# Mixed attention's differential units: the relative bias is added by VectorE within its row maxima, instead of by TensorE with identity products

## The chip, the cores and the metric

The kernel runs on one core of a Trainium2 chip. The metric is the device time of one execution in microseconds (us): the median of several. A core has four engines that compute: TensorE (PE: matrix products into the PSUM memory, with a separate part that loads weights, PEld), VectorE (DVE), ScalarE (ACT) and GpSimd (POOL); SyncE (SP) issues DMA transfers. Each engine works through its own list of instructions in order, and waits for others through semaphores.

## What is computed

Two model blocks follow each other on 256 tokens of width 1024. The first has four layers (dilated attention twice, a short convolution, a conformer convolution, each with a gated feed-forward part). The second adds 16 meta tokens (272 keys) and has a feed-forward part, a mixed attention and another feed-forward part. The change lies in the mixed attention, in its differential half:

```python
bias = bias_a[rel_bucket(q_pos[:, None], k_pos[None, :])].transpose(2, 0, 1)
s = jnp.einsum('bqhmd,bkhmd->bhmqk', q[:, start:stop], k[:, :stop]).astype(jnp.float32)
s = s * A_SCALE + bias[None, :, None].astype(jnp.float32)
s = jnp.where(k_pos[None, :] <= q_pos[:, None], s, -jnp.inf)
p = jax.nn.softmax(s, axis=-1)
a = p[:, :, 0] - lam * p[:, :, 1]
outs.append(jnp.einsum('bhqk,bkhd->bqhd', a.astype(v.dtype), v[:, :stop]))
```

Each of 4 heads has two maps of scores (m = 0, 1) that share one bias; both get a softmax, and their difference weighs the values. The other half of the mixed attention (4 latent heads) works on keys picked by an index and has one map a head.

## The kernel before

Almost all time is matrix products of activations with weights. The weights are streamed from HBM in slabs, and each slab is split by ScalarE (L1260) and VectorE (L1689) into a high and a low part, so that three fast products (L2304 to L2306) give fp32 accuracy. The phases stand in one list (`phases`), and every engine's program runs over it; the order within a phase is written out by hand, the same on each engine's side.

The mixed attention is the phase `mix2`. It has 16 units: n = 0 to 7 are differential, n = 8 to 15 latent. `unit(n)` gives the query block q (units 0 to 3 and 8 to 11 are q = 0 with w = 144 keys, the others q = 1 with w = 272) and the head. Three buffers of scores in PSUM (`SCORE_BANK`, two banks for a differential unit, one a map) and three buffers of weights in SBUF (`expd`) are used in turn. For a differential unit n:

- `mix_scores` (TensorE): for each map a product of the identity with the bias table `rel2` (fp32, in SBUF; it holds bias and causal mask), L901, and on top of it the product of queries and keys, L905. A product of fp32 operands shows as two passes in the profile, so a unit has four rows of either line.
- `mix_max` (VectorE): one reduction over both maps gives the negative row maxima, L921.
- `mix_exps` (ScalarE): the exponential of each map, from PSUM into `expd`, with the row sums, L941.
- `weigh` (VectorE): reciprocals (L1002), times lambda (L1003, L1004), and the difference of the maps (L1005).
- `turn` (TensorE): two or three transposes with the identity, L1078; `turned_copy` (ScalarE): their copy to SBUF, L954.
- `values` (TensorE): the product with the values, L1095; `clamp` (VectorE): its bounded copy, L1013.

In the loop over n, VectorE does the maxima of unit n + 1, the weights of unit n, for n below 5 two steps of the index selection of the latent half (`select`, L819 to L823), then the clamp of unit n - 1. At n = 5 a reciprocal (L1044) stands ahead of the clamp. TensorE does the scores of unit n + 2, the values of unit n - 1 and the transposes of unit n. ScalarE does the exponentials of unit n + 1 and the copy of unit n's transposes. GpSimd makes eight sums of bias and selection for the latent units (L2271) as soon as the selection is there. Unit 0's scores, maxima and exponentials and unit 1's scores stand in the phase before, `heads`, between its last matrix products.

Latent units have their scores at L910, an add of the bias at L926, maxima at L929, and the values' product at L1097. The dilated attention of the first block has, at L559, a `tensor_tensor_reduce` that adds a mask to scores in PSUM, writes the negative sum to SBUF and takes the minimum of each row.

Of the kernel before, what the change touches and what calls it, by code (L numbers as in the profile page):

```python
# [23 lines left out]
ALU = mybir.AluOpType  # L24
ACT = mybir.ActivationFunctionType
AX = mybir.AxisListType.X
# [4 lines left out]
TW = SEQ + META  # L31
# [134 lines left out]
def build(nc, A, out):  # L166
# [81 lines left out]
    s = 0  # L248
# [59 lines left out]
    with ExitStack() as ctx:  # L308
        def sb(name, shape, dt=F32):
            return ctx.enter_context(nc.sbuf_tensor(name, shape, dt))  # L310

        def sem(name):
            return ctx.enter_context(nc.semaphore(name))
# [9 lines left out]
        rel2 = res[:].rearrange("p (h t) -> p h t", t=TW)  # L323
# [17 lines left out]
        def put(name, shape, offset, dt=F32):  # L341
            return nc.alloc_sbuf_tensor_at(name, shape, dt, offset=offset)
# [45 lines left out]
        z = put("z", [P, 20, TW], R_Q)  # L388
# [15 lines left out]
        ident = sb("ident", [P, P])  # L404
# [33 lines left out]
        ps = ctx.enter_context(nc.psum_tensor("ps", [P, 8, 512], F32))  # L438
# [16 lines left out]
        relw_ready, rel_done, skew_ready, skew_stored, bias_landed = (  # L455
            sem("relw_ready"), sem("rel_done"), sem("skew_ready"), [sem(f"skew_stored{j}") for j in range(2)],
            sem("bias_landed"))
# [42 lines left out]
        s2_done, s2_biased, s2_max, s2_exp, s2_prob = (  # L500
            sem("s2_done"), sem("s2_biased"), sem("s2_max"), sem("s2_exp"), sem("s2_prob"))
        t2_done, t2_copied, o2_done = sem("t2_done"), sem("t2_copied"), sem("o2_done")
# [122 lines left out]
        expd = [[tmp1[:, 2 * b + m, :] for m in range(2)] for b in range(3)]  # L625
# [14 lines left out]
        s2_negmax = [mstat[:, 40 + 2 * b:42 + 2 * b] for b in range(3)]  # L640
# [116 lines left out]
        def unit(n):  # L757

            return (n % 8) // 4, n % 4
# [131 lines left out]
        def mix_scores(pe, n):  # L891
            q, head = unit(n)
            w, bank = KEYS[q], SCORE_BANK[n % 3]
            if n == 0:
                pe.wait_ge(bias_landed, 32)
                pe.wait_ge(vl_copied, 3)
            if n >= 3:
                pe.wait_ge(s2_exp, n - 2)
            if n < 8:
                for m in range(2):  # L900
                    pe.matmul(ps[:, bank + m, 0:w], ident[:], rel2[:, head, TW - w:TW], start=True, stop=False,  # L901
                              skip_group_check=True)
                for m in range(2):
                    rows = slice(m * HD, (m + 1) * HD)
                    mm = pe.matmul(ps[:, bank + m, 0:w], z[rows, head, META + q * P:META + (q + 1) * P],  # L905
                                   z[rows, 4 + head, 0:w], start=False, stop=True, skip_group_check=True)
            else:
                pe.wait_ge(ckey_ready, 2)
                for k in range(2):
                    mm = pe.matmul(ps[:, bank, 0:w], qlat[:, 2 * head + k, q * P:(q + 1) * P], ckey[:, k, 0:w],  # L910
                                   start=(k == 0), stop=(k == 1))
            mm.then_inc(s2_done, 1)

        def mix_max(dve, n):
            q, head = unit(n)
            w, b, bank = KEYS[q], n % 3, SCORE_BANK[n % 3]
            dve.wait_ge(s2_done, n + 1)
            if n >= 3:
                dve.wait_ge(s2_exp, n - 2)
            if n < 8:  # L920
                dve.tensor_reduce(s2_negmax[b], ps[:, bank:bank + 2, 0:w], AX, ALU.max, negate=True).then_inc(s2_max, 1)  # L921
                return
            dve.wait_ge(bsel_ready, n - 7)
            dve.wait_ge(t2_done, n - 2)
            s = expd[b][0][:, 0:w]
            dve.scalar_tensor_tensor(out=s, in0=ps[:, bank, 0:w], scalar=rq[:, n - 8:n - 7], in1=bsel[:, n - 8, 0:w],  # L926
                                     op0=ALU.mult, op1=ALU.add).then_inc(s2_biased, 1)
            dve.wait_ge(s2_biased, n - 7)
            dve.tensor_reduce(s2_negmax[b][:, 0:1], s, AX, ALU.max, negate=True).then_inc(s2_max, 1)  # L929

        def mix_exps(act, n):
            q, _ = unit(n)
            w, b, bank = KEYS[q], n % 3, SCORE_BANK[n % 3]
            act.wait_ge(s2_max, n + 1)
            if n == 0:
                act.wait_ge(rq_sum, 1)
            if n >= 3:
                act.wait_ge(t2_done, n - 2)
            for m in range(2 if n < 8 else 1):
                src = ps[:, bank + m, 0:w] if n < 8 else expd[b][0][:, 0:w]  # L940
                e = act.activation(expd[b][m][:, 0:w], src, ACT.Exp, bias=s2_negmax[b][:, m:m + 1],  # L941
                                   accum_out=s2_sum[b][:, m:m + 1])
            e.then_inc(s2_exp, 1)

# [48 lines left out]
        def mix2_vector(dve, B, link):  # L993
# [39 lines left out]
            for n in range(16):  # L1033
                if n + 1 < 16:
                    mix_max(dve, n + 1)
                weigh(n)
                if n == TURN_BY_DVE:
                    turned_copy(dve, n).then_inc(t2_copied, 1)
                if n < 5:
                    for step in range(9 + 2 * n, min(11 + 2 * n, SEL_STEPS)):  # L1040
                        select(dve, step)
                if n == 5:
                    dve.wait_ge(rq_root, 1)
                    link(dve.reciprocal(rq, rq_std))  # L1044
                if 1 <= n <= 8:
                    clamp(n - 1)
                if n == 9:
                    dve.wait_ge(oa_sq, 8)
                    dve.tensor_scalar(oa_std, oa_sum, 1.0 / P, 1e-6 * OA_SCALE ** 2, ALU.mult, ALU.add).then_inc(oa_var, 1)
                if n == 10:  # L1050
                    dve.wait_ge(oa_root, 1)
                    link(dve.reciprocal(oa_rstd, oa_std))
                    link(dve.scalar_tensor_tensor(out=oa_rstd, in0=oa_std, scalar=OA_STD_MAX, in1=oa_rstd, op0=ALU.is_lt,
                                                  op1=ALU.mult))
                if n >= 13:
                    low_a(2 * (n - 13))
                    low_a(2 * (n - 13) + 1)
                if 10 <= n < 14:
                    scale_a(2 * (n - 10))
                    scale_a(2 * (n - 10) + 1)  # L1060
                if n >= 10:
                    low_b(n - 2)
# [5 lines left out]
        def mix2_tensor(pe, B):  # L1068
# [40 lines left out]
            for n in range(16):  # L1109
                if n + 2 < 16:  # L1110
                    mix_scores(pe, n + 2)
                if n == 0:
                    turn_values(pe, 2, B_heads)
                    turn_values(pe, 3, B_heads)
                if n:
                    values(n - 1)
                turn(n)
                if n >= 12:
                    turn_a(2 * (n - 12))
                    turn_a(2 * (n - 12) + 1)  # L1120
# [102 lines left out]
        def _(act):  # L1223
# [62 lines left out]
            for ph in phases:  # L1286
# [270 lines left out]
                elif ph.kind == "heads":  # L1557
                    for m in range(4 * ph.n):
# [29 lines left out]
                        if m == 15:  # L1588
                            latent_std(act)
                            load_table(act, ACT.Exp)  # L1590
                            mix_exps(act, 0)
# [10 lines left out]
        def _(dve):  # L1602
# [169 lines left out]
            for ph in phases:  # L1772
# [126 lines left out]
                elif ph.kind == "heads":  # L1899
# [7 lines left out]
                    for m in range(4 * ph.n):  # L1907
# [26 lines left out]
                        if m == 15:  # L1934
                            mix_max(dve, 0)
# [340 lines left out]
        def _(pe):  # L2276
# [80 lines left out]
            for ph in phases:  # L2357
# [263 lines left out]
                elif ph.kind == "heads":  # L2621
                    for m in range(4 * ph.n):
# [19 lines left out]
                        if m == 12:  # L2642
                            latent_query(pe, 6, B)
                            latent_query(pe, 7, B)
                            head_spreads(pe, 6)
                            head_spreads(pe, 7)
                        elif m == 13:
                            for k in range(3):
                                latent_values(pe, k)
                        elif m == 14:  # L2650
                            latent_sums(pe)
                            mix_scores(pe, 0)
                        elif m == 15:
                            turn_values(pe, 0, B)
                            turn_values(pe, 1, B)
                            pe.wait_ge(drained_a, B["da"] + 8)
                            mix_scores(pe, 1)
# [144 lines left out]
```

## Time and profile before

| | |
|---|---|
| median of 3 runs | 2153.34 us (2152.84 to 2155.52) |
| the profiled execution's own time | 2155.34 us |
| its span (first to last instruction) | 2153.5 us |
| mean granted clock of TensorE | 0.995 of full |
| TensorE busy | 2115.3 us (98%) |
| VectorE, ScalarE, GpSimd busy | 1477.2, 1018.1, 481.8 us |

The differential units lie between about 1885 and 1912 us from the start of the span, and the mixed attention ends at about 1932. Busy times are sums over the whole program; which engine sets the pace in a stage is read from its own stretch, and from the chain of waits, which is followed back from the last instruction: at each step to what released it, or to the instruction before it on its engine. A matrix product's bar overlaps that of the next one, and a VectorE bar overlaps the start of the next by some 0.08 us.

### The profile page before, as it was taken

How to read it: one execution, taken by the hardware profiler on the slowest of the kernel's cores; microseconds unless marked ns; L12 is line 12 of the kernel's file. 1: busy time of each engine (PE TensorE's matmuls, PEld its weight loads, DVE VectorE, ACT ScalarE, POOL GpSimd, SP SyncE). 2: the span in 40 equal slices, each digit the busy share in tenths (PEclk: the TensorE clock that was granted, in tenths of full speed). 3: DMA queues.
4: the chain of work that ended last, by engine and by line, in shares of the span. 5: the costliest groups of instructions: out<-in, count | busy, mean ns of one | idle time of the engine just before them, and what ended most of it. 6: DMA issues, size and time to landing. Idle time of an engine off the chain costs nothing.

```text
span 2153.5 us, 43259 instructions
## 1 busy us (share of the span) xinstructions
PE 2115.3 (98%) x16233; PEld 1935.1 (90%) x16240; DVE 1477.2 (69%) x2516; ACT 1018.1 (47%) x1376; POOL 481.8 (22%) x518
## 2 busy tenths in 40 slices
PE   8999999999999999999999999999999999999999
PEld 7997779989999888799889987799889998779998
DVE  7884778857688667688678847788565545586653
ACT  4335765544455443455543346655453334364342
POOL 3220005510135314044212200054113300201320
PEclk9999999999999999999999999999999999999999
DMA  5555235565645654245645563255655555305554
GB/s 184 192 177 185 89 124 175 190 202 174 211 138 192 202 161 148 69 158 193 208 154 190 180 190 104 97 181 181 200 163 171 172 172 178 98 21 176 181 182 144
DMA packets 300950, 350.37 MB, mean 163 GB/s; under 512 B 7604, under 2 KB 255990, under 8 KB 300854
## 3 DMA queue, kind: packets, MB, share of 16 engines
q1 hardware_dynamic: 295318, 344.45, 49.4%
q10 hardware_dynamic: 5152, 4.37, 0.7%
q8 instruction: 64, 1.05, 0.2%
q0 software_dynamic: 384, 0.24, 0.0%
q14 instruction: 32, 0.26, 0.0%
HBM read 346.35 MB, written 2.68 MB: 162 GB/s over the span
## 4 chain that ended last, share of the span: by engine, by line
PE 90%; DVE 4%; ACT 4%; issue 1%; DMA 0%; ACTq 0%; DVEq 0%
PE ps L2304 26%; PE ps L2306 26%; PE ps L2305 26%; PE ps L2731 2%; DVE w_lo L1689 2%; ACT w_hi L1260 1%; PE ps L2441 1%; PE ps L2436 1%; PE ps L2437 1%; ACT prob L566 1%; PE ps L2668 1%; PE ps L2373 1%; PE ps L2681 1%; PE ps L2316 1%; PE ps L2282 0%
## 5 line engine op out<-in xcount | busy, mean ns | idle before, releaser
L1689 DVE TENSOR_TENSOR w_lo<-raw,w_hi 128x2048 fp32r<-128x2048 f32 (+3 forms) x311 | 695.8, 2237 | 452.3 <-ACT w_hi L1260 452.2
L2304 PE MATMUL ps<-a_hi,w_hi 128*128 128x256 f32 (+1 forms) x3200 | 907.8, 284 | 6.3 <-DVE w_lo L1689 4.5
L2306 PE MATMUL ps<-a_hi,w_lo 128*128 128x256 f32 (+1 forms) x3200 | 904.4, 283 | 0.0
L2305 PE MATMUL ps<-a_lo,w_hi 128*128 128x256 f32 (+1 forms) x3200 | 904.2, 283 | 0.0
L1260 ACT CAST w_hi<-raw 128x2048 fp32r<-128x2048 f32 (+3 forms) x319 | 589.3, 1847 | 540.6 <-PE ps L2306 526.6
L2304 PEld LDWEIGHTS ps<-a_hi,w_hi 128*128 128x128 f32 x3200 | 605.8, 189 | 13.2 <-DVE w_lo L1689 6.4
L2306 PEld LDWEIGHTS ps<-a_hi,w_lo 128*128 128x128 f32 x3200 | 606.6, 190 | 0.0
L2305 PEld LDWEIGHTS ps<-a_lo,w_hi 128*128 128x128 f32 x3200 | 603.4, 189 | 0.4 <-issue 0.2
L2209 POOL TENSOR_TENSOR hs<-sg,cv 128x256 f32<-128x256 f32 x88 | 65.4, 743 | 644.4 <-DVE cv L2046 644.4
L2216 POOL CAST hid_hi<-hs 128x256 f32 (+3 forms) x132 | 137.9, 1045 | 297.0 <-DVE hs L2092 282.7
L2304 PE MATMUL ps<-w_hi,hid_hi 128*128 128x512 f32 x480 | 189.5, 395 | 2.3 <-DVE w_lo L1685 1.2
L2306 PE MATMUL ps<-w_hi,hid_lo 128*128 128x512 f32 x480 | 189.2, 394 | 0.0
L2305 PE MATMUL ps<-w_lo,hid_hi 128*128 128x512 f32 x480 | 188.4, 392 | 0.0
L1466 ACT ACTIVATE cv<-ps,par 128x256 f32<-128x256 f32 x176 | 82.1, 475 | 209.4 <-DVE ps L1735 205.1
L2046 DVE SCALAR_TENSOR_TENSOR cv<-ps,par,cv 128x255 f32<-128x255 f32 (+1 forms) x352 | 152.2, 477 | 27.1 <-ACT cv L1466 23.4
L2218 POOL TENSOR_TENSOR hid_lo<-hs,hid_hi 128x256 f32 (+3 forms) x132 | 138.1, 1046 | 20.9 <-POOL hid_hi L2216 19.9
L2248 POOL TENSOR_TENSOR qk<-rope_cos,rope_sin 128x256 f32 x96 | 79.0, 823 | 274.0 <-DVE rope_sin L1747 274.0
L1735 DVE TENSOR_TENSOR ps<-ps,rpre 128x256 f32<-128x256 f32 (+1 forms) x244 | 103.3, 429 | 36.4 <-PE ps L2306 30.2
L2304 PE MATMUL ps<-hid_hi,w_hi 128*128 128x256 f32 (+1 forms) x416 | 118.1, 284 | 0.3 <-DVE w_lo L1689 0.3
L2306 PE MATMUL ps<-hid_hi,w_lo 128*128 128x256 f32 (+1 forms) x416 | 117.9, 283 | 0.0
L2305 PE MATMUL ps<-hid_lo,w_hi 128*128 128x256 f32 (+1 forms) x416 | 117.6, 283 | 0.0
L2304 PEld LDWEIGHTS ps<-w_hi,hid_hi 128*128 128x128 f32 x480 | 90.2, 188 | 23.8 <-DVE w_lo L1685 2.0
(357 smaller groups left out, 2558.0 us busy)
## 6 DMA issues: line engine op xcount, KB each, us to landing
raw<-in_ffn_w_in_dram SPq DMA_DIRECT2D x88, 1024.0 KB, 5.1
raw<-in_attn_w_qkv_dram SPq DMA_DIRECT2D x71, 1024.0 KB, 5.1
raw<-in_ffn_w_out_dram SPq DMA_DIRECT2D x32, 1024.0 KB, 5.1
raw<-in_ffn_w_gate_dram SPq DMA_DIRECT2D x22, 1024.0 KB, 5.3
raw<-in_ffn_w_up_dram SPq DMA_DIRECT2D x22, 1024.0 KB, 5.3
raw<-in_ffn_w_down_dram SPq DMA_DIRECT2D x16, 896.0 KB, 4.9
raw<-in_sc_w_in_dram SPq DMA_DIRECT2D x12, 1024.0 KB, 5.2
raw<-in_ffn_w_out_dram SPq DMA_DIRECT2D x16, 768.0 KB, 4.5
```

Of the source, the lines that this page charges most:

```text
L1260: act.copy(o, src).then_inc(hi_ready, 1)
L1466: act.activation(cv[:, j, :], ps[:, j, 0:SEQ], ACT.Copy, scale=g).then_inc(tap_ready, 1)
L1689: dve.tensor_tensor(o, src, hi.bitcast(F32), ALU.subtract).then_inc(lo_ready, 1)
L1735: dve.tensor_tensor(tile, tile, rpre[:, 0:w], ALU.mult).then_inc(scaled, 1)
L2046: return dve.scalar_tensor_tensor(out=cv[:, j, back:SEQ], in0=ps[:, j, 0:SEQ - back], scalar=g, in1=cv[:, j, back:SEQ], op0=ALU.mult, op1= ...
L2209: pool.tensor_tensor(hs[:, j, 0:w], sg[:, j, 0:w], cv[:, 2 + j, :], ALU.mult).then_inc(hid_mul, 1)
L2216: pool.tensor_copy(hi, hs[:, j, 0:w]).then_inc(hid_hi_ready, 1)
L2218: pool.tensor_tensor(lo, hs[:, j, 0:w], hi.bitcast(F32), ALU.subtract).then_inc(hid_ready, 1)
L2248: pool.tensor_tensor(o, rope_cos[:, j, :], rope_sin[:, j, :], ALU.add).then_inc(rope_ready, 1)
L2304: pe.matmul(o, wh, xh, start=start, stop=False)
L2305: pe.matmul(o, wh, xl, start=False, stop=False)
L2306: return pe.matmul(o, wl, xh, start=False, stop=stop)
```

## The change

The identity products and TensorE's wait for the bias table are gone; queries times keys start the sum. VectorE runs, for each map, a `tensor_tensor_reduce` that reads the scores from PSUM and the bias from SBUF, writes -(scores + bias) into `expd` and the smallest value of each row into `s2_negmax`. It waits for the bias table at unit 0, and from unit 3 on for the transposes of unit n - 3, which read the same buffer. ScalarE's exponential reads `expd` in place with scale -1.

```diff
@@ mix_scores @@
             if n == 0:
-                pe.wait_ge(bias_landed, 32)
                 pe.wait_ge(vl_copied, 3)
             if n >= 3:
                 pe.wait_ge(s2_exp, n - 2)
             if n < 8:
                 for m in range(2):
-                    pe.matmul(ps[:, bank + m, 0:w], ident[:], rel2[:, head, TW - w:TW], start=True, stop=False,
-                              skip_group_check=True)
-                for m in range(2):
                     rows = slice(m * HD, (m + 1) * HD)
                     mm = pe.matmul(ps[:, bank + m, 0:w], z[rows, head, META + q * P:META + (q + 1) * P],
-                                   z[rows, 4 + head, 0:w], start=False, stop=True, skip_group_check=True)
+                                   z[rows, 4 + head, 0:w], start=True, stop=True, skip_group_check=True)
@@ mix_max @@
             if n < 8:
-                dve.tensor_reduce(s2_negmax[b], ps[:, bank:bank + 2, 0:w], AX, ALU.max, negate=True).then_inc(s2_max, 1)
+                if n == 0:
+                    dve.wait_ge(bias_landed, 32)
+                if n >= 3:
+                    dve.wait_ge(t2_done, n - 2)
+                for m in range(2):
+                    biased = dve.tensor_tensor_reduce(expd[b][m][:, 0:w], ps[:, bank + m, 0:w], rel2[:, head, TW - w:TW], -1.0,
+                                                      3.0e38, ALU.add, ALU.min, s2_negmax[b][:, m:m + 1])
+                biased.then_inc(s2_max, 1)
                 return
@@ mix_exps @@
             for m in range(2 if n < 8 else 1):
-                src = ps[:, bank + m, 0:w] if n < 8 else expd[b][0][:, 0:w]
-                e = act.activation(expd[b][m][:, 0:w], src, ACT.Exp, bias=s2_negmax[b][:, m:m + 1],
+                s = expd[b][m][:, 0:w]
+                e = act.activation(s, s, ACT.Exp, scale=-1.0 if n < 8 else 1.0, bias=s2_negmax[b][:, m:m + 1],
                                    accum_out=s2_sum[b][:, m:m + 1])
```

## Rows read from the trace of the kernel before

**Rows 1.** The page: the chain that ended last, share of the span by engine.

```profile
PE 90%; DVE 4%; ACT 4%; issue 1%; DMA 0%; ACTq 0%; DVEq 0%
```

**Rows 2.** Stretches: length, PE, PEld, DVE, ACT, POOL busy (count), PEclk, DMA share, GB/s.

```profile
1890.95:1904.50 13.55, 12.29 (x71) 7.95 (x71) 13.02 (x54) 8.12 (x32) 0.00 (x0) 1.00 0.00 1
1904.50:1910.50 6.00, 5.07 (x30) 3.60 (x30) 5.16 (x16) 3.47 (x14) 5.02 (x8) 1.00 0.00 0
```

**Rows 3.** The chain by line, from 1890.95 to 1910.50 and from 1910.50 to 1932.40.

```profile
by line: DVE mstat L921 16.2%; DVE tmp L1004 12.9%; DVE tmp L1005 12.8%; DVE chosen L823 12.3%; DVE top L821 11.3%; DVE mstat L1003 6.9%; issue 5.7%; PE ps L1095 5.5%; PE ps L901 4.7%; PE ps L905 3.4%; DVE tmp L1013 3.4%; DVE mstat L1002 2.
...
by line: PE ps L1097 31.9%; PE ps L1078 15.1%; PE ps L910 14.8%; ACT tmp L954 11.2%; PE ps L1095 10.3%; issue 4.1%; DVE mstat L929 2.0%; DVE tmp L954 1.9%; DVE tmp L926 1.9%; DVE tmp L1016 1.4%; DVE tmp L1009 1.4%; PE ps L1105 1.0%; DVE hid
```

**Rows 4.** The chain in order of time: start us, us, what.

```profile
1889.96 0.49 PE ps L901 x4
...
1904.49 0.49 PE ps L1078 x3
1904.99 0.92 PE ps L901 x4
...
1906.57 1.07 PE ps L1095 x6
...
1909.01 0.93 DVE tmp L1004
...
1911.05 0.49 ACT tmp L954
```

**Rows 5.** Waits of TensorE, whole program: us in total, times, longest.

```profile
PE ps L1078 <- DVE tmp L1005: 1.7, 3, 0.9
```

**Rows 6.** VectorE in order of time: start, us, line, operation, [idle before <- releaser].

```profile
1890.95 0.46 DVE L921 TENSOR_REDUCE mstat<-ps 128x2 f32<-128x288 f32 x1 [0.38 <-PE ps L905]
...
1893.62 0.45 DVE L921 TENSOR_REDUCE mstat<-ps 128x2 f32<-128x288 f32 x1
1893.99 0.15 DVE L1002 RECIPROCAL mstat<-mstat 128x2 f32<-128x2 f32 x1
...
1899.34 0.71 DVE L921 TENSOR_REDUCE mstat<-ps 128x2 f32<-128x544 f32 x1
1899.97 0.15 DVE L1002 RECIPROCAL mstat<-mstat 128x2 f32<-128x2 f32 x1
...
1906.91 0.19 DVE L1044 RECIPROCAL mstat<-mstat 128x8 f32<-128x8 f32 x1
1907.73 0.29 DVE L1013 TENSOR_SCALAR tmp<-ps 128x128 f32<-128x128 f32 x1 [0.63 <-PE ps L1095]
```

**Rows 7.** VectorE in the dilated attention, in order of time.

```profile
232.56 0.56 DVE L559 CUSTOM_DVE_ANT_0 prob<-ps,maskb 128x384 f32<-128x384 f32 x1 [0.58 <-PE ps L2324]
...
233.05 0.55 DVE L559 CUSTOM_DVE_ANT_0 prob<-ps,maskb 128x384 f32<-128x384 f32 x1
233.53 0.08 DVE L559 DVE_READ_ACCUMULATOR2_ANT cols<- 128x1 f32 x1
233.53 0.16 DVE L572 RECIPROCAL cols<-cols 128x1 f32<-128x1 f32 x1
```

**Rows 8.** Groups by line and shape, VectorE: count, busy us, mean ns, idle.

```profile
L1005 DVE SCALAR_TENSOR_TENSOR tmp<-tmp,mstat 128x272 f32<-128x272 f32 x4 | 2.1, 531 | 0.1
...
L926 DVE SCALAR_TENSOR_TENSOR tmp<-ps,mstat,bsel 128x272 f32<-128x272 f32 x4 | 2.0, 490 | 0.0
```

**Rows 9.** Line L941 on ScalarE: count, ns min/median/max, first and last start.

```profile
L941 ACT ACTIVATE tmp<-ps,mstat x16: 371/430/488, 1889.0 to 1909.2; 128x144 f32<-128x144 f32 x8, 128x272 f32<-128x272 f32 x8
...
L941 ACT ACTIVATE tmp<-tmp,mstat x8: 398/468/539, 1911.7 to 1927.4; 128x144 f32<-128x144 f32 x4, 128x272 f32<-128x272 f32 x4
```

**Rows 10.** VectorE's L1004 and GpSimd's last sum in order of time.

```profile
1903.54 0.36 DVE L1004 TENSOR_SCALAR tmp<-tmp,mstat 128x272 f32<-128x272 f32 x1
...
1909.01 0.76 POOL L2271 TENSOR_TENSOR bsel<-res,tmp 128x272 f32<-128x272 f32 x1
```

**Rows 11.** A stretch of the first block, columns as in rows 2.

```profile
302.50:305.00 2.50, 1.62 (x9) 1.23 (x9) 0.88 (x3) 1.79 (x5) 0.00 (x0) 0.77 0.29 110
```

## The prediction

> **What bounds the kernel now.** I read the page first. The chain that ended last is 90% TensorE [rows 1], so this is a TensorE-bound kernel with short stretches in which another engine sets the pace. The change touches one stage only, the 16 units of the mixed attention, so I asked next which engine paces that stage. The table of stretches shows VectorE busy for 13.02 of the 13.55 us from 1890.95 on, and for 5.16 of the next 6.00, while ScalarE has 8.12 and 3.47 [rows 2]. TensorE looks nearly as full there, 12.29 and 5.07, and a reader who stops at this table may think that work taken from it is worth its whole time. The chain of waits decides. By line it is almost all VectorE from 1890.95 to 1910.50: the row maxima (L921) alone are 16.2% of it, the identity products (L901) 4.7%; from 1910.50 to 1932.40 it is TensorE's, with the products of values (L1095, L1097), the transposes (L1078) and the scores of the latent units (L910), none of which the change touches [rows 3]. In order of time the identity products are on the chain in two places: just ahead of 1890.95, where unit 1's maxima wait for its scores, and at 1904.99, for unit 7 [rows 4]. Between them TensorE waits for VectorE instead: its transposes (L1078) stood idle until L1005 had written the weights, 3 times and 1.7 us in all [rows 5].
>
> **What it takes from TensorE.** Each differential unit loses two fp32 products with the identity, recorded as four passes: 0.49 us for 144 keys (units 0 to 3) and 0.92 us for 272 (units 4 to 7) [rows 4]. That is 4 x 0.49 + 4 x 0.92 = 5.6 us of TensorE in all. It is the most that the change can bring, and only if every pass were on the path.
>
> **What it adds to VectorE.** Before: one reduction over both maps. It keeps the engine 0.37 us at 144 keys (1893.62 until the reciprocal behind it starts, 1893.99) and 0.63 us at 272 (1899.34 to 1899.97) [rows 6]. After: two fused add-and-reduce instructions, one a map, each followed by a read of the accumulator. The trace has this pair, in the dilated attention at L559: it starts every 0.485 us at 384 keys, and the accumulator read (0.08 us) starts together with the instruction behind it, the next fused one or the reciprocal [rows 7], so in VectorE's time it is free. The size of one at 144 and 272 keys is my estimate: the reductions cost 0.63 - 0.37 = 0.26 us more for 2 x 128 more elements, thus 1.02 ns an element; then 384 elements are 0.39 us and 0.09 are fixed, and one fused instruction costs 0.24 us at 144 keys and 0.37 at 272, two cost 0.48 and 0.74. Added: 0.11 us a unit in either half; since bars and starts are rounded I count +0.10, between +0.09 and +0.11.
>
> One thing of L559 differs: its second operand is bf16 and here it is fp32. The nearest rows are L926, with one operand in PSUM and an fp32 one in SBUF (490 ns at 272), and L1005, with two fp32 ones in SBUF (531 ns, among them one lengthened by something else) [rows 8]. The two are close, so I take full rate; half rate is the upper bound and a rival below. The Trainium skill, "Vector Engine (DVE) Microarchitecture Reference", section "Points that are easy to get wrong", warns that the scalar-tensor-tensor shape with two SBUF sources that aren't bf16 runs at half throughput. The trace doesn't bear that out for L1005, and here one source is PSUM anyway; if it did hold for the new form, the sum would be that of the rival.
>
> **What follows on ScalarE.** The exponentials now read SBUF instead of PSUM: L941's two forms have medians of 430 and 468 ns, about +0.03 each [rows 9]. They start later behind the start of the maxima: the second accumulator read must end (0.08). At 144 keys that is 0.24 + 0.24 + 0.11 = 0.59 us against 0.46 + 0.03 before. Unit n+1's exponentials are made while VectorE is still on unit n, and ScalarE is busy 8.12 of 13.55 us, so some +0.2 us a unit is hidden; were the cover gone, it would be about 1 us over five units.
>
> **The waits that move.** VectorE's new wait for the transposes of unit n-3 (it now overwrites their source) stands behind work on unit n-2, whose output it has already used in the clamp: never late, 0. The wait for the bias table moves from TensorE to VectorE, which had it in the selection long before: 0. No DMA, and nothing on GpSimd's or SP's queue, changes.
>
> **The sum, from the start of the stage to its end.**
> (a) Unit 1's maxima start at 1890.95 after 0.38 us of idle that TensorE's L905 ended, and a row starts some 0.08 us before the bar ahead of it is over, so 0.46 can go. TensorE is by then two identity groups earlier (0.49 each), more than enough. But unit 0's maxima, ahead on VectorE, are 0.10 longer. Net -0.36.
> (b) Units 1 to 5: five times +0.10 on VectorE's own chain, +0.50. Unit 4's weights, and with them the transposes at 1904.49, come at -0.36 + 0.50 = +0.1.
> (c) From 1904.49 the path ran over TensorE: transposes, identity, scores, values, and then the clamp (L1013) at 1907.73 after 0.63 us of idle [rows 4, 6]. Without the identity, the copy of the transposes (ScalarE's L954, 0.49 like the one at 1911.05) is the longer branch beside the scores, and the clamp could start at 1904.6 + 0.49 (transposes) + 0.49 (copy) + 1.07 (values) and some hand-overs, about 1907.0. VectorE itself is then the later one: its reciprocal L1044 stood at 1906.91 and moves to 1907.11 (+0.1 of (b), +0.1 for unit 6's maxima), and the clamp follows about 0.23 later, 1907.34: -0.4 against 1907.73.
> (d) Unit 7's maxima, +0.1: -0.3.
> (e) Now something eats it. L1004 at 1909.01 is 0.93 us of the chain, against 0.36 at 1903.54 for the same shape, and it ended just after GpSimd's last sum (L2271, from 1909.01 for 0.76) [rows 4, 10]. GpSimd's eight sums start when the selection is done, after unit 5's maxima, so they come 0.1 us later, not earlier, while L1004 comes 0.3 earlier, in the middle of the sum before the last. If VectorE gets its turn between the two sums, L1004 ends about 0.55 earlier, but L1005 behind it may meet the last one; if not, L1004 ends 0.1 later than now. Bounds for the whole up to here: -0.55 and +0.1. I take -0.2.
> The Trainium skill, "SBUF — State Buffer", section "SBUF: two separate sides", says that VectorE and GpSimd share one port pair by an exclusive lock, for two-port modes and for VectorE operations with two SBUF inputs. L1004's row agrees. By that rule the new instructions, with one source in PSUM, would not take part; if they did, it is a rival below.
> (f) From 1910.52 the path is TensorE's and ScalarE's and has no part in the change; then follow dense matrix products to the end. Whatever (e) gives goes through: -0.2 us.
>
> The profiled execution took 2155.34 us with a span of 2153.5, so 1.8 lie around the span; its sum is 2155.1. The median of the runs shown is 2153.34, so I predict **2153.1 us**: no change. About 0.2% (4.3 us) is what a measurement of this kernel can tell from no change; -0.2 us is far below.
>
> **Rivals.**
> 1. TensorE's clock falls (the other side). In units 1 to 5 the idle of TensorE grows by 0.5 to 1.0 us each, its busy time in the first stretch falls from 12.29 by 0.49 + 3 x 0.92 to 9.0 of 13.55 us. For: from 302.50 to 305.00 the mean granted clock was 0.77, between the full 2.4 GHz and the 1.2 GHz level, with TensorE busy for 1.62 of 2.50 [rows 11]: about the same share. Against: it is 1.00 all through the stage now, and no new gap is much over 1.3 us. It costs little while VectorE paces; it decides if it lasts beyond 1910.50. There 73% of 21.9 us, 16 us, are TensorE's on the path [rows 3]. The products with 272 columns (L910, 3.2 us) would double at 1.2 GHz; the 128-column ones, which carry a weight load each, anything from nothing to half again: +3 to +9, typically +6: 2159. Chance 5%.
> 2. The fp32 operand is read at half rate. +0.15 us for each instruction at 144 and +0.28 at 272, thus +0.9 for units 1 to 3 and +2.3 for units 4 to 7, on the chain that VectorE paces: +3 us, 2156.3. Against it stands L926. Chance 5%.
> 3. The fused instructions get into GpSimd's way: units 6 and 7 have their maxima while its sums run, each of the four could wait up to 0.76: +1 us typically, 2154.3. Chance 8%.
> 4. TensorE was the true bound, and the waits ascribed to VectorE hide it: all 5.6 us come, 2147.7. Against: rows 5, and VectorE busy 13.02 of 13.55. Chance 3%.
> The forecast itself, a few tenths either way, has 79%.
>
> **The numbers.** Faster by over 0.2% is rival 4: 0.03. Slower by over 0.2% is most of rival 1 and a tail of rival 2: 0.05. Within: 0.92. The three runs before already lie between 2152.84 and 2155.52, so the range is made by them and rivals 2 and 3: 2151.0 to 2156.3.
>
> **What would show it.** After: L901 gone; two fused instructions a unit at about 300 and 430 ns, starting 0.24 and 0.37 us apart; unit 1's maxima without idle before them; the transposes L1078 waiting for L1005 longer than 1.7 us in all; the table switch at 1932.41 a few tenths earlier; the clock 1.00 through the stage. I am wrong if VectorE's maxima take over 0.9 us a unit at 272 keys, if the clock row falls, or if the stage is shorter by over 1 us, which would mean that TensorE, not VectorE, paced it.

## The result, and the profile after

The changed kernel takes 2163.59 us (median of 6 runs, 2159.6 to 2168.76) against 2154.1 for the kernel before (6 runs, 2151.07 to 2155.61): a ratio of 1.0044, interval 1.0033 to 1.0054, thus 9.5 us slower. Its profiled execution took 2162.31 us, with a span of 2160.5 (before: 2153.5) and a mean granted clock of 0.988 (before: 0.995). The chain of the page hardly moved, and says nothing of the cause [rows 1]:

```profile
PE 90%; DVE 5%; ACT 4%; issue 1%; DMA 0%; ACTq 0%; DVEq 0%
```

The stage tells more. The changed kernel's lines have other numbers: L922 is the fused instruction, L901 is now the product of queries and keys (L905 before), L906 the latent scores (L910), L1005 the reciprocals (L1002), L1007 and L1008 the weights (L1004, L1005), L1016 the clamp (L1013), L1081 the transposes (L1078), L1098 the values (L1095). VectorE of the changed kernel in order of time: units 1 and 4, as [rows 6] shows them before.

```profile
1890.79 0.30 DVE L922 CUSTOM_DVE_ANT_0 tmp<-ps,res 128x144 f32<-128x144 f32 x1
1891.02 0.08 DVE L922 DVE_READ_ACCUMULATOR2_ANT mstat<- 128x1 f32 x1
1891.02 0.30 DVE L922 CUSTOM_DVE_ANT_0 tmp<-ps,res 128x144 f32<-128x144 f32 x1
...
1891.24 0.16 DVE L1005 RECIPROCAL mstat<-mstat 128x2 f32<-128x2 f32 x1
...
1899.45 0.43 DVE L922 CUSTOM_DVE_ANT_0 tmp<-ps,res 128x272 f32<-128x272 f32 x1
1899.81 0.08 DVE L922 DVE_READ_ACCUMULATOR2_ANT mstat<- 128x1 f32 x1
1899.81 0.43 DVE L922 CUSTOM_DVE_ANT_0 tmp<-ps,res 128x272 f32<-128x272 f32 x1
...
1900.17 0.16 DVE L1005 RECIPROCAL mstat<-mstat 128x2 f32<-128x2 f32 x1
```

The pair keeps VectorE for 0.45 us at 144 keys (1890.79 to 1891.24) and 0.72 at 272 (1899.45 to 1900.17), against 0.37 and 0.63 before; there is no idle ahead of unit 1's. Unit 4's weights (L1008) start at 1904.22, against 1903.93 before: 0.3 later where 0.1 was forecast, and 0.2 of that is a later start of the whole stage in this trace. Up to here the kernel is close to the forecast. TensorE isn't. Stretches of the changed kernel (columns as in rows 2):

```profile
1890.00:1892.50 2.50, 1.30 (x12) 0.90 (x10) 2.39 (x13) 2.11 (x9) 0.00 (x0) 1.00 0.01 5
1892.50:1895.00 2.50, 1.73 (x10) 1.06 (x10) 2.39 (x14) 1.77 (x7) 0.00 (x0) 1.00 0.02 7
1895.00:1897.50 2.50, 1.82 (x10) 1.04 (x10) 2.43 (x15) 1.23 (x7) 0.00 (x0) 0.99 0.00 0
1897.50:1900.00 2.50, 1.97 (x8) 0.83 (x7) 2.46 (x12) 1.25 (x6) 0.00 (x0) 0.50 0.00 0
...
1922.50:1925.00 2.50, 2.50 (x7) 1.36 (x6) 0.00 (x0) 2.45 (x5) 0.00 (x0) 0.55 0.03 7
1925.00:1927.50 2.50, 1.79 (x10) 1.20 (x9) 1.84 (x8) 1.49 (x5) 0.00 (x0) 1.00 0.00 0
```

and the same of the kernel before:

```profile
1890.00:1892.50 2.50, 2.50 (x21) 1.90 (x20) 2.02 (x8) 1.44 (x6) 0.00 (x0) 1.00 0.00 0
1892.50:1895.00 2.50, 2.17 (x17) 1.55 (x15) 2.39 (x11) 2.07 (x7) 0.00 (x0) 1.00 0.00 0
1895.00:1897.50 2.50, 2.50 (x15) 1.49 (x14) 2.43 (x12) 1.27 (x6) 0.00 (x0) 1.00 0.00 0
1897.50:1900.00 2.50, 2.44 (x14) 1.45 (x13) 2.46 (x11) 1.07 (x5) 0.00 (x0) 1.00 0.00 0
```

Read the column before the last two, the granted clock. It was 1.00 in every stretch of this stage; now it falls to 0.50, which is 1.2 instead of 2.4 GHz, at about 1897.5 and comes back at about 1925. Ahead of the fall TensorE was busy for 1.30, 1.73 and 1.82 of 2.50 us where it had 2.50, 2.17 and 2.50. A busy time of 2.50 afterwards is no sign of health: it is the same work, stretched. TensorE of the changed kernel in order of time, with its waits (last bracket), around the fall and where it matters:

```profile
1891.02 0.52 PE L901 MATMUL ps<-z 64*128 64x144 f32 x4 [1.00 <-DVE work L1907]
...
1895.20 0.39 PE L1081 MATMUL ps<-ident,tmp 128*16 128x128 f32 x2 [0.68 <-DVE tmp L1008]
1895.51 0.73 PE L901 MATMUL ps<-z 64*128 64x272 f32 x4
1896.73 0.88 PE L1098 MATMUL ps<-va,tmp 16*128 16x128 f32 x4 [0.49 <-DVE tmp L1016]
1898.15 0.60 PE L1081 MATMUL ps<-ident,tmp 128*16 128x128 f32 x2 [0.54 <-DVE tmp L1008]
1898.67 1.28 PE L901 MATMUL ps<-z 64*128 64x272 f32 x4
...
1904.78 0.81 PE L1081 MATMUL ps<-ident,tmp 128*16 128x128 f32 x3 [0.17 <-DVE tmp L1008]
...
1906.73 1.94 PE L1098 MATMUL ps<-va,tmp 16*128 16x128 f32 x6
1908.46 0.85 PE L1081 MATMUL ps<-ident,tmp 128*16 128x128 f32 x3
1909.10 1.17 PE L906 MATMUL ps<-tmp,qlat 128*128 128x144 f32 x4
...
1922.14 2.02 PE L906 MATMUL ps<-tmp,qlat 128*128 128x272 f32 x4
...
1925.35 1.08 PE L906 MATMUL ps<-tmp,qlat 128*128 128x272 f32 x4
```

Of the kernel before, unit 5's values and the block of scores that answers to the one at 1925.35:

```profile
1906.50 1.12 PE L1095 MATMUL ps<-va,tmp 16*128 16x128 f32 x6
...
1918.38 1.08 PE L910 MATMUL ps<-tmp,qlat 128*128 128x272 f32 x4
```

The transposes that took 0.49 us [rows 4] take 0.81 to 0.85, the same scores of 272 keys 1.28 against 0.73 ahead of the fall, the products of values 1.94 against 1.12. From 1905 until 1925 TensorE no longer waits for anyone, so every stretched product is paid. The waits for L1008 got shorter, not longer: 1.4 us in all against 1.7 [rows 5], because from 1905 on it is TensorE that comes late.

```profile
PE ps L1081 <- DVE tmp L1008: 1.4, 3, 0.7
```

From the transposes of unit 4 (1904.78, before 1904.49) to the second block of scores with 272 latent keys (1925.35, before 1918.38) TensorE needs 20.57 us instead of 13.89: +6.68. With the 0.29 by which it starts later that is the whole delay. The end of the stage is ScalarE's table switch ahead of the dense products; in the changed kernel, and then in the kernel before:

```profile
1939.38 1.28 ACT L754 ACT_TABLE_LOAD   x1
```

```profile
1932.41 1.28 ACT L754 ACT_TABLE_LOAD   x1
```

That is 6.97 later, and the span is 7.0 longer: outside the stage the two runs take the same time in sum. The median's 9.5 is more than this profiled run's 7.0; the six runs have mean clocks from 0.989 to 0.983, and the profiled one (0.988) is among the faster.

### The profile page after: what moved, and what is told of

It reads as the page before. It is cut to its first block, busy times and chain, and to the rows that moved or that the text cites. A ratio compares the mean times of both kernels' runs of the same rounds, so it can differ in the third digit from the quotient of the medians.

```text
span 2160.5 us, 43226 instructions
## 1 busy us (share of the span) xinstructions
PE 2121.6 (98%) x16208; PEld 1939.3 (90%) x16208; DVE 1478.8 (68%) x2540; ACT 1018.4 (47%) x1376; POOL 481.8 (22%) x518
## 4 chain that ended last, share of the span: by engine, by line
PE 90%; DVE 5%; ACT 4%; issue 1%; DMA 0%; ACTq 0%; DVEq 0%
PE ps L2307 26%; PE ps L2309 26%; PE ps L2308 26%; PE ps L2734 2%; DVE w_lo L1692 2%; ACT w_hi L1263 1%; PE ps L2444 1%; PE ps L2439 1%; PE ps L2440 1%; ACT prob L566 1%; PE ps L2376 1%; PE ps L2671 1%; PE ps L2684 1%; PE ps L2319 1%; PE ps L2285 0%
```

## The experiments

Theory C, the first rival: VectorE's new form costs what was forecast, and the loss comes from TensorE's clock, which falls because the identity products are gone. Theory V: the loss is in the new instructions, their SBUF traffic or their waits, and the clock is a symptom. To compare stages, I take the time from unit 0's reciprocals (L1002 before, L1005 after) to that table switch in the profiled run. "Clock" is the lowest stretch in it. The ratios are those recorded with each comparison, to runs of the kernel before made beside it (medians 2155.43 us for e1 to e4, 2155.14 for e5 to e8, 2153.67 for e9 and e10), and not quotients of two medians.

| kernel | median us (runs) | ratio to before | stage us | clock |
|---|---|---|---|---|
| before | 2154.1 (6) | 1 | 41.08 | 1.00 |
| changed | 2163.59 (6) | 1.0044 [1.0033, 1.0054] | 48.14 | 0.50 |
| e1 changed, products put back, idle | 2153.82 (12) | 0.9995 [0.9986, 1.0004] | 41.39 | 1.00 |
| e2 before, products left out | 2162.07 (11) | 1.0041 [1.0028, 1.0053] | 51.82 | 0.50 |
| e3 changed, waits filled, three | 2154.52 (12) | 0.9995 [0.9985, 1.0005] | 41.41 | 1.00 |
| e4 change in units 0 to 3 only | 2154.66 (12) | 0.9992 [0.9982, 1.0002] | 41.27 | 1.00 |
| e5 changed, waits filled, one | 2157.02 (11) | 1.0014 [1.0003, 1.0025] | 56.77 | 0.50 |
| e6 change in units 4 to 7 only | 2163.94 (5) | 1.0037 [1.0023, 1.0051] | 50.13 | 0.50 |
| e7 as e3, other waits filled too | 2150.0 (11) | 0.9979 [0.9970, 0.9988] | 41.40 | 1.00 |
| e8 before, other waits filled, lambda folded | 2149.32 (7) | 0.9973 [0.9962, 0.9984] | 39.73 | 1.00 |
| e9 as e7, lambda folded | 2149.99 (11) | 0.9985 [0.9976, 0.9994] | 44.64 | 0.50 |
| e10 before, other waits filled | 2149.82 (11) | 0.9983 [0.9974, 0.9992] | 41.10 | 1.00 |

**e1: the identity products put back, without use.** The scores start their sum anew over them, so VectorE's and ScalarE's work is all the changed kernel's.

```diff
                 for m in range(2):
+                    pe.matmul(ps[:, bank + m, 0:w], ident[:], rel2[:, head, TW - w:TW], start=True, stop=True,
+                              skip_group_check=True)
+                for m in range(2):
                     rows = slice(m * HD, (m + 1) * HD)
                     mm = pe.matmul(..., start=True, stop=True, skip_group_check=True)
```

> The changed kernel with the identity products put back on TensorE as idle work: each is written first and then overwritten by the scores (start=True), so VectorE still adds the bias. Theory C (TensorE's granted clock fell because the stage lost these products): the clock is 1.00 all through the mixed attention, the fused instructions keep their 300 and 430 ns, and the time is 0.998 to 1.002 of before (2152 to 2158 us). Theory V (the new form on VectorE and ScalarE is what costs): it stays at 1.004, some +9 us. Theory D (the clock falls in this stage by chance of how runs fall, not for the products): the clock row falls here too in the profile.

2153.82 us, no different from before, with the clock at 1.00 throughout the stage. Theory V would have kept the loss, since all of VectorE's new work is in it. Doing 5.6 us of useless products on TensorE gives back some 10 us (2153.82 against 2163.59). The profiled run is the fastest of the 12, and so is e3's; but all runs of both have mean clocks of 0.993 to 0.998, like the kernel before beside them, where the changed kernel has 0.983 to 0.989.

**e2: the products taken out, and nothing else.** VectorE and ScalarE are those of the kernel before; bias and mask are left out of the differential units.

```diff
-                for m in range(2):
-                    pe.matmul(ps[:, bank + m, 0:w], ident[:], rel2[:, head, TW - w:TW], start=True, stop=False,
-                              skip_group_check=True)
...
-                                   z[rows, 4 + head, 0:w], start=False, stop=True, skip_group_check=True)
+                                   z[rows, 4 + head, 0:w], start=True, stop=True, skip_group_check=True)
```

> The kernel before with only the identity products taken out; VectorE keeps its one reduction from PSUM, ScalarE its exponentials from PSUM. Left out of the computation: bias and causal mask of the differential units. Theory C: the clock falls to 0.50 in the stage as in the changed kernel and the time is +5 to +12 us, though VectorE has no more work than before. Theory V: no loss, 2153 to 2155, perhaps 0.4 us faster for the later start.

2162.07 us: nearly the whole loss without one new VectorE instruction. Its stretches, at a lowered clock from 1892.5 until about 1931:

```profile
1890.00:1892.50 2.50, 1.77 (x10) 1.04 (x10) 2.43 (x12) 1.22 (x6) 0.00 (x0) 1.00 0.00 0
1892.50:1895.00 2.50, 2.04 (x9) 0.99 (x8) 2.46 (x10) 1.13 (x5) 0.00 (x0) 0.66 0.00 0
1895.00:1900.00 5.00, 4.88 (x17) 2.77 (x16) 4.79 (x21) 2.87 (x11) 0.19 (x1) 0.50 0.00 2
...
1930.00:1935.00 5.00, 4.30 (x26) 2.98 (x24) 3.23 (x12) 2.58 (x12) 0.00 (x0) 0.92 0.00 0
```

**e3 and e5: other work in TensorE's waits.** Three, or one, bf16 products of 128 x 512 ahead of the transposes of units 1 to 5, into PSUM bank 6, which these transposes then overwrite. The edit of e3; e5 has `range(1)`.

```diff
                 if n:
                     values(n - 1)
+                if 1 <= n <= 5:
+                    for _ in range(3):
+                        pe.matmul(ps[:, 6, 0:512], identb[:], maskb[:, 0:512], start=True, stop=True,
+                                  skip_group_check=True)
                 turn(n)
```

> The changed kernel with three bf16 products of 512 columns (some 0.65 us) put into TensorE's wait ahead of the transposes of units 1 to 5, into the PSUM bank that the transposes overwrite. Theory C: the clock stays at 1.00 and the time is that of before or up to 0.5 us less (0.998 to 1.001), as the filling lies where TensorE waited. If the place of the work matters and not its amount, the clock could still fall between the scores. Theory V: 1.004.

> As e3, with one bf16 product of 512 columns (0.21 us) in each of the five waits instead of three. Theory C with a wide margin: still 1.00 and the time of before (0.998 to 1.001). Theory C with a narrow margin (TensorE was barely busy enough before): the clock falls again, in all or some of the executions, 1.002 to 1.005. Any rival that holds the fill to be a matter of waits rather than of work done would see no difference between this and e3.

With three, 2154.52 and the clock at 1.00: it isn't the identity products that TensorE needs, nor their place ahead of the scores, but something to do while it waits. Stretches of e3:

```profile
1890.00:1895.00 5.00, 4.03 (x23) 2.15 (x22) 4.86 (x27) 2.54 (x11) 0.00 (x0) 1.00 0.02 5
1895.00:1900.00 5.00, 3.98 (x23) 1.89 (x23) 4.82 (x22) 2.98 (x12) 0.33 (x1) 1.00 0.00 0
```

With one, nine of 11 runs took 2154.87 to 2159.13 us, at mean clocks of 0.991 to 0.993, and two took 2166.89 and 2167.38, at 0.985. The profiled one was of the two, and its clock stayed low from 1895 to about 1946:

```profile
1890.00:1895.00 5.00, 3.20 (x18) 1.51 (x17) 4.86 (x25) 2.57 (x12) 0.00 (x0) 1.00 0.00 0
1895.00:1900.00 5.00, 4.82 (x16) 2.68 (x16) 4.79 (x24) 3.30 (x13) 0.00 (x0) 0.53 0.00 2
```

So one product is at the edge: the same program spent some 50 us at the low clock in the profiled run and took about 10 us less in most of the others. Even these have a lower mean clock than e3's runs (0.995 to 0.998).

**e4 and e6: half of the change.** Units 0 to 3 take the fused form and the others keep the identity products, and the other way round; the edit is a condition on n in the three functions of the diff, here that of e4.

```diff
+                if n >= 4:
+                    for m in range(2):
+                        pe.matmul(ps[:, bank + m, 0:w], ident[:], rel2[:, head, TW - w:TW], start=True, stop=False,
+                                  skip_group_check=True)
...
-                                   z[rows, 4 + head, 0:w], start=True, stop=True, skip_group_check=True)
+                                   z[rows, 4 + head, 0:w], start=(n < 4), stop=True, skip_group_check=True)
```

> The change for units 0 to 3 only (144 keys); units 4 to 7 (272 keys) keep identity products, one reduction and exponentials from PSUM. Theory C: the identity products of units 4 to 7 are issued from 1895 on, so TensorE's busy time in the stretch 1894 to 1904 is as before; if that holds the clock, the time is 0.999 to 1.001. If the loss ahead of 1895 (four groups of 0.49 us) already suffices, the clock falls as in the changed kernel. Theory V: half of the 9 us, 1.002.

> The mirror of e4: the change for units 4 to 7 only, where each unit loses 0.92 us of TensorE's work, from 1895 on; units 0 to 3 keep the identity products. Theory C: TensorE is short of work between 1895 and 1905 exactly as in the changed kernel, so the clock falls there, perhaps later, and the time is 1.002 to 1.005. If the four groups ahead of 1895 count as well (clock falls only when both are gone), it is 0.999 to 1.001.

e4 is 2154.66 and its clock stays at 1.00; e6 is 2163.94 in 5 runs, a ratio of 1.0037 and so nearly the whole loss. The small products (0.49 us a unit) can go alone, the large ones (0.92) can't. Stretches of e4, and then of e6:

```profile
1890.00:1895.00 5.00, 3.00 (x20) 1.96 (x20) 4.79 (x26) 3.85 (x15) 0.00 (x0) 1.00 0.02 5
1895.00:1897.50 2.50, 2.34 (x13) 1.43 (x13) 2.43 (x15) 1.24 (x6) 0.00 (x0) 1.00 0.00 0
```

```profile
1890.00:1895.00 5.00, 4.67 (x36) 3.45 (x34) 4.41 (x18) 3.50 (x13) 0.00 (x0) 1.00 0.00 0
1895.00:1897.50 2.50, 2.01 (x12) 1.11 (x11) 2.43 (x12) 1.27 (x6) 0.00 (x0) 1.00 0.00 0
1897.50:1900.00 2.50, 2.05 (x8) 0.94 (x8) 2.46 (x12) 1.07 (x5) 0.00 (x0) 0.57 0.00 0
```

The busy share alone doesn't sort them: e4 was idle for 2.0 of the first 5 us and stayed at 1.00, e6 for 0.33 and fell soon after, behind a stretch with 2.01 of 2.50. What exactly the chip counts stays open; that less work for TensorE in this stage is what makes it fall is shown by e1, e2, e3 and e6 from four sides.

**e7 to e10: the same remedy where the kernel before has a low clock.** The mean clock of before is 0.995, not 1. In its trace it is below 1 in five short places outside this stage (around 22 to 32, 302 to 307, 497 to 502, 1797 to 1802 and 1812 to 1817 us), each at a wait of TensorE. Filling them was tried with the changed kernel (e7) and with that of before (e10), and both also with one VectorE instruction less a unit (e9, e8). `warm_up` runs the same product; 17 stand ahead of the second slab (21 us), 4 each at the start of two feed-forward parts (304 and 498), 10 ahead of the latent keys and 7 ahead of the last heads. e7 and e9 have e3's fills as well.

```diff
+                        if not n:
+                            warm_up(17)
...
+                    if n and tok and pre.prior in gaps:
+                        for _ in range(4):
+                            pe.matmul(ps[:, 0, :], identb[:], maskb[:, 0:512], start=True, stop=True)
...
+                    for _ in range(10):
+                        pe.matmul(ps[:, 4, :], identb[:], maskb[:, 0:512], start=True, stop=True)
                     pe.wait_ge(ik_lo, 1)
...
+                    for _ in range(7):
+                        pe.matmul(ps[:, 4, :], identb[:], maskb[:, 0:512], start=True, stop=True)
                     for m in range(4 * ph.n):
```

```diff
-                    link(dve.tensor_scalar(s2_lam[b], s2_rinv[b][:, 1:2], lam, None, ALU.mult))
-                    link(dve.tensor_scalar(e[1], e[1], s2_lam[b], None, ALU.mult))
+                    link(dve.tensor_scalar(e[1], e[1], s2_rinv[b][:, 1:2], lam, ALU.mult, ALU.mult))
```

> e3 with idle bf16 products also in the five other long waits of TensorE after which the profile shows the half clock: 17 at 21 us (the wait for the second slab), 4 in each of the two feed-forward starts at 304 and 498 us, 10 ahead of 1798 and 7 ahead of 1811 us. Theory C: the clock is 1.00 in all of these, each stretch at half clock (some 3 to 6 us long, thus 1.5 to 3 us lost) is gone, and the time is 5 to 9 us below before: 0.996 to 0.998. If the idle products delay what they precede, or the clock falls for another reason, 0.999 or more.

> The kernel before (identity products kept, no fill in the mixed attention) with the idle products of e7 in the five other waits, and one small VectorE instruction less in each differential unit: lambda is multiplied in the same instruction as the reciprocal (L1003 goes, 0.25 us with its wait, on the path for units 0 to 4). Theory C: as e7, and about 1.2 us less: 2145 to 2149, 0.995 to 0.998. If the two-scalar form leaves the fast mode, L1004 grows by some 0.15 us a unit and half of the 1.2 us is lost.

> The changed kernel with three small products in each of TensorE's five waits of the stage, the products that fill the five other waits of TensorE (ahead of the second slab, at the start of two feed-forward parts, ahead of the latent keys and of the last heads), and lambda folded into the weights (L1006 and L1007 become one tensor_scalar with two scalars, one VectorE instruction less a unit). Theory C (only the clock made the changed kernel slower; with the clock held the change itself is worth next to nothing): the same as the kernel before with the same fills and the same fold, within 1 us, thus 2148.5 to 2150, against its fellow e10 0 to 1.5 us less. Rival (identity products were worth their time once VectorE is relieved by the fold): TensorE's 0.5 to 0.9 us a unit come back as well, and it is 2 us or more below the same kernel with the products (2147 or less).

> The kernel before with the products that fill its five waits outside the stage, and nothing else. If the fills alone explain the gain of the kernel with fills and folded lambda (2149.3), this one is at 2149 to 2150.5 and the stage's table switch stays near 1927.9 or 1928; if the folded lambda brings its 0.2 us a unit to the end, this one is 0.8 to 1.5 us above its fellow e9 and above 2150. The other reading, that the run-to-run spread of the kernel before (2151 to 2156) has another source than these falls of the clock, expects a spread of 3 us or more here too.

All four beat the kernel before, by 0.15 to 0.27%; their intervals overlap, so none is shown to be the best. The fills did not end all falls: in its profiled run e8 still has 0.65 and 0.67 between 495 and 500, one of the filled places, and e7's clock goes down to 0.50 at a new one, between 1877.5 and 1885, just ahead of the stage; e10's is at 1.00 until TensorE's work ends. e8, at 2149.32, missed its forecast of at most 2149 by a little.

The gain is that of the fills: e10, with nothing else, has 0.9983 and mean clocks of 0.998 to 1. The fold takes 1.37 us out of e8's stage (39.73 against e10's 41.10), but by the median it is 0.5 us, within the scatter; my expectation that e10 would lie 0.8 us above its fellow e9 failed (2149.82 and 2149.99). The profiled run of e9, the slowest of its 11, shows one reason: the clock fell within the stage. Its stretches, and then TensorE's wait ahead of unit 6's transposes, where nothing fills it:

```profile
1902.50:1905.00 2.50, 1.69 (x10) 1.34 (x11) 2.39 (x7) 1.26 (x6) 0.38 (x1) 0.93 0.00 0
1905.00:1907.50 2.50, 2.50 (x12) 2.15 (x12) 1.29 (x6) 0.88 (x4) 0.00 (x0) 0.50 0.00 0
```

```profile
1903.23 0.50 PE L1080 MATMUL ps<-ident,tmp 128*16 128x128 f32 x3 [0.78 <-DVE tmp L1007]
```

It was back to 1.00 by 1915. That this wait is what brought the clock down isn't shown: the kernel before waits at the same place for longer, with the clock at 1.00 throughout.

```profile
1910.52 0.50 PE L1078 MATMUL ps<-ident,tmp 128*16 128x128 f32 x3 [0.88 <-DVE tmp L1005]
```

The same kernel with this wait filled wasn't tried. The runs of before also show what the other dips cost: in the last comparison its 21 runs go from 2150.33 us (mean clock 0.997) to 2157.36 (0.993), and the slower ones are with few exceptions those with the lower clock. So most of the kernel's own scatter goes with the clock. With the five places filled, e10's 11 runs lie between 2148.95 (clock 1.000) and 2152.41 (0.998). That is 3.5 us, half of the 7.0 beside it, but still over the 3 us that the other reading of e10's expectation had named; what is left again goes with the clock.

## Why the prediction was wrong

Forecast: no change, 2153.1, with 5% for a fall of the clock. Measured: 9.5 us slower, by that very rival.

**The step that failed** is that the sum holds TensorE's clock at 1.00, and with it the weighing of rival 1: "Against: it is 1.00 all through the stage now, and no new gap is much over 1.3 us." Both halves are true, and neither is evidence. That the clock was full with TensorE busy 12.29 of 13.55 us [rows 2] says nothing of 9.0 (or of 8.6: the 9.0 leaves out unit 2's identity products, which start at 1890.83). And the gaps needn't be long: the longest ahead of the fall were 1.00, 0.68 and 0.49 us. The profile had a number that spoke for it, and I had copied it: 0.77 at a busy share of 1.62 in 2.50 [rows 11]. After the change the shares were 1.30, 1.73 and 1.82.

How much that number was worth could have been read too. Cut the trace of the kernel before into stretches of 2.5 us. At each of its five falls of the clock TensorE was busy for 0.00 to 1.64 us of the stretch in which the clock fell or of the one ahead of it. But five other stretches (from 232.5, 242.5, 280, 885 and 1317.5) have 1.56 to 1.84 and no fall in them or behind them, for example:

```profile
1317.50:1320.00 2.50, 1.56 (x35) 1.39 (x36) 2.43 (x10) 1.81 (x6) 0.00 (x0) 1.00 1.09 376
```

By these ten places a fall was about as likely as not; that is an estimate, and e4 (1.27 and 1.73 in two stretches running, and no fall) shows again that the share decides it only in part. I had worked out that the stage would come to two thirds, named a stretch of this kernel with two thirds and a fallen clock, and still gave it 5%.

**Its price** was of the right kind and a little small: "+3 to +9, typically +6", against 7.0 in the profiled run and 9.5 by the median, just above the upper end. The term that was too low is that for the 128-column products, "anything from nothing to half again": at 0.50 they took 1.7 times as long (0.85 for 0.49, 1.94 for 1.12), though each has a weight load beside it. "It decides if it lasts beyond 1910.50": it did, to about 1925.

**The sum, with the clock held** (e1, e3), is 0.31 and 0.33 us longer than before, where the forecast comes to +0.06 in this measure (-0.2 at the end, and unit 0's reciprocals, where it starts, 0.36 - 0.10 = 0.26 earlier). By steps:

- (a) No idle ahead of unit 1's maxima, right. They are 0.16 earlier rather than 0.36; the whole stage starts 0.2 later in this trace.
- (b) +0.10 a unit: measured 0.08 and 0.09. In e3 the transposes behind unit 4's weights come at +0.38 in this measure, forecast +0.40. Right, and full rate for the fp32 operand (rival 2 wrong): 0.36 us from one to the next at 272 keys.
- (c), (d) wrong. The clamp should have come 0.4 earlier, -0.14 in this measure. In e3 it comes at +0.46 (1902.73 against 1907.73, with the reciprocals at 1885.87 and 1891.33), because unit 5's weights take longer beside GpSimd's sums. VectorE of e3, units 5 and 6, then GpSimd of e3, then unit 5 of the kernel before:

```profile
1900.99 0.67 DVE L1007 TENSOR_SCALAR tmp<-tmp,mstat 128x272 f32<-128x272 f32 x1
1901.70 0.89 DVE L1008 SCALAR_TENSOR_TENSOR tmp<-tmp,mstat 128x272 f32<-128x272 f32 x1
...
1904.10 0.70 DVE L1007 TENSOR_SCALAR tmp<-tmp,mstat 128x272 f32<-128x272 f32 x1
```

```profile
1899.67 4.97 POOL L2278 TENSOR_TENSOR bsel<-res,tmp 128x144 f32<-128x144 f32 x8 [32.22 <-DVE tmp L819]
```

```profile
1905.98 0.36 DVE L1004 TENSOR_SCALAR tmp<-tmp,mstat 128x272 f32<-128x272 f32 x1
1906.38 0.61 DVE L1005 SCALAR_TENSOR_TENSOR tmp<-tmp,mstat 128x272 f32<-128x272 f32 x1
```

Together they take 1.56 us instead of 0.97. They ran beside GpSimd's sums in the kernel before as well, whose first sum starts at 1904.75; only 0.09 us lie between the two cases (L1004 starts 1.23 behind that sum, L1007 of e3 1.32 behind it), and e1 and the changed kernel show the long form too (0.67 and 0.88). I had looked for this meeting only at unit 6, where it was on the chain (e): there it became 0.22 shorter (0.70 for 0.92). The maxima themselves are not lengthened by GpSimd: in e3 those of units 6 and 7, 0.43 each, start 0.36 and 0.35 apart, so rival 3 didn't happen, but its mechanism did, one line further. The Trainium skill, "SBUF — State Buffer", section "SBUF: two separate sides", has the exclusive lock, shared with GpSimd, for VectorE operations with two SBUF inputs; the runs agree for L1008 (0.89 beside the sums, 0.50 without) and for the fused form, which has one source in PSUM (0.43 either way). L1007, with one tile as input, is lengthened all the same (0.67 and 0.70 for 0.36); the section names two-port modes beside, and no run here tells whether L1007 is in one.
- (f) Right as a statement of where the path is: TensorE's. It is why the clock could take all it took.

**Rival 4**, that all 5.6 us come: wrong. With the clock held, the stage without the identity products (e3) is as long as with them (e1), 41.41 and 41.39 us, and e10's, with them on the old path, is the shortest of the three (41.10). They stood in TensorE's waits.

**The other signs.** "The transposes waiting longer than 1.7 us in all" failed (1.4) for a reason that itself pointed to the cause; I had called "the clock 1.00 through the stage" a sign, and it was the one that settled it.

## What to carry to other kernels

Work on TensorE that stands in its waits is not free to remove: where another engine paces, work out how busy TensorE would still be, look in the same trace for all stretches like it, with a fallen clock and without, and let their number set the chance (here about one in two by the ten places, where the forecast had 5%). The price is paid not in that stretch but in the next, where TensorE is the path and the clock is still low. Before removing such work, or where the clock row shows less than 1.00, put a few idle products into the waits: 15 of them turned 2163.6 into 2154.5 here, and 42 in other waits gained 0.2% on the kernel before.

## What was unexpected of the hardware

- The clock stayed at 0.50 for 27 us in the changed kernel, about 50 in e5's profiled run and 10 in e9's, while the rows show TensorE busy for nearly all of the time. In the changed kernel and e9 it came back within the same transposes and fp32 products (1925 and 1915), in e5 only when the dense products had begun (about 1946).
- At 0.50 every kind of product of the stage is lengthened by 1.7 to 1.9: transposes 0.85 for 0.49, values 1.94 for 1.12, latent scores of 144 keys 1.17 for 0.66, of 272 keys 2.02 for 1.08.
- The margin is narrow: three idle products a unit (0.71 us, e3) held the clock in all 12 runs, one did not in 2 of 11, which took over 10 us more than the median of the other nine.
- The fused add-and-reduce with an fp32 operand in SBUF and one in PSUM starts every 0.23 us at 144 and every 0.36 us at 272 elements.
